# Dealing the merge products differently over eight samples, with one output weight kept in the gates' buffer

## The chip, the cores and the metric

The kernel runs on one core of one Trainium2 chip. The metric is the device time of one execution in microseconds. Before the change three runs took 859.84 us (median), 859.52 and 865.72 us. A separate profiled execution took 862.67 us, with a span of 861.0 us from its first to its last instruction.

## The reference

One inference step of a decoder layer over 272 prompt rows (16 of them meta tokens) and 8 samples of 8 new tokens each. A token mixer has two branches: a recurrent one, A, and softmax attention, B. Each sample attends over 2048 cached positions, which lie in 16 pages. Then comes a mixture of 32 experts, two per token.

```
z = xn @ w_in                                # among others the gates ga, gb: 1024 columns each
merged = sigmoid(ga) * (oa @ proj_a) + sigmoid(gb) * (ob @ proj_b)
h = h + merged @ w_out                       # w_out: 1024 x 1024
h = h + hier_moe(rms_norm(h, ln2_w))         # 32 experts, w1, w3: 1024 x 256, w2: 256 x 1024
y = rms_norm(h, ln_f)
```

The last layer drops the meta tokens, so 256 prompt tokens and 64 sample tokens go through the merge: 320 columns.

## The kernel before

The program is a row of blocks with a barrier between them. This case is about the block `cache` (from L1703), which attends from the samples to their cached pages and, in between, merges the two branches of the prompt. The block after it runs the experts.

**Memory.** One on-chip buffer, `arena`, is cut into weight slots of 128 x 2048 floats (1 MB), named by `place[n]`. The DMA queue of SyncE (SP) fills most of them, and the queue of GpSimd (POOL) loads the cached values. Keys of a sample come as 16 pages of 256 KB into slots 0 to 3 (even samples) or 11 to 14 (odd ones), values as 16 pages into slots 4 to 7. A slot is loaded again as soon as its last reader is done.

**A round of TensorE (PE).** For each sample b the PE queue holds: `scores(b+1)` (L1837, L1854, L1860, L1863); `turn_out(b-1)` (L1912); `turn_probs(b)` (L1880, L1883); `weigh(b)`, the probabilities times the values (L1897, L1906), in four quarters that each wait for four value pages; and then `fills(b+1)`, some of the merge products. In the last round, b = 7, the fills stand ahead of `weigh(7)` instead, behind four turns of the sample tokens' gates (L1980).

**The merge products.** There are 32, in the order of the list `kinds`: 8 of kind "a" (320 columns, four matmuls each, L1938), gated with A's gates into `mT`; 8 of kind "b" (256 columns), gated with B's gates and added to `mT`; 16 of kind "o" (two matmuls of 512 columns in the program, L1927), a quarter of `w_out` (c = 0 to 3) times `mT`, added to `h2`. A float32 matmul of the program is two in the trace, so a product of kind "a" or "b" counts x8 there and one of kind "o" x4. They alternate between two banks of PSUM, so product f waits until VectorE (DVE) has emptied product f-2; the semaphore is `fill_sb`. `turn_probs(b)` uses the same banks and waits for all products so far. `m_ready` counts finished columns of `mT`; the first "o" product waits for all eight.

The table `fill_no` deals them out; its line before, L1676, is `fill_no = [0, 0, 5, 8, 11, 14, 18, 24, 28, len(kinds)]`. `fills(n)` runs the products from entry n to entry n+1, so the rounds get 5, 3, 3, 3, 4, 6, 4 and 4 of them, the last four in round 7.

**DVE** works in a fixed order as well: for sample b the maxima of the scores (L2255), `turn_bias` (L2174), `keep_out(b-2)` (L2213, on which `weigh(b-1)` waits), two key transposes for b+1 (L1590), the sums of the exponentials once ScalarE (ACT) is done with them (L2272), `scale_out(b-1)` (L2206), the outputs of the products `fills_out(b)` (L2239 for "a", L2241 and L2243 for "b", L2233 for "o"), and two transposes for b+2.

**The gates.** The pre-sigmoid gates wait in DRAM as `gates_dram`, (2, 128, 8, 320). `gates_load(a)` brings one branch's into `gates`, 128 x 2560 floats, 10 KB in a row; ACT applies the sigmoid (L2082) in its own order, between the probabilities of sample b and the exponentials of b+1 (L2112), for b = 0 and b = 2. POOL keeps the sample tokens' part aside (L1812) behind its last value pages; PE's turns at L1980 wait for that.

**Output weights.** `out_load(c)` (L1605) brings quarter c of `w_out` into slot 16, 10, 0 or 1. Slots 0 and 1 hold keys of sample 6 until `scores(6)`. The same four slots serve once more at L2039, for the sample tokens.

**After the rounds.** PE turns the normalised tokens (`turn_x2`, L1994), computes the router and the samples' part (L2008 to L2039) and enters the expert block, where 81 more loads of 1 MB run through the slots; `ahead(sp, s)` has filled the 18 slots before with the first expert weights.

Of the kernel before, what the change touches and what calls it, by code (L numbers as in the profile page):

```python
# [12 lines left out]
DM, SEQ, NMETA, HD = 1024, 256, 16, 64  # L13
# [12 lines left out]
P = 128  # L26
# [4 lines left out]
TM = T - NMETA  # L31
# [9 lines left out]
SLOTS, SLOT = 8, 2048  # L41
# [54 lines left out]
def build(nc, A, O):  # L96
# [17 lines left out]
    with ctx:  # L114
# [21 lines left out]
        xnT = keep(KT, T)  # L136
# [1470 lines left out]
        gates = xnT.rearrange("p k t -> p (k t)")[:, 0:DM // P * TM].rearrange("p (d t) -> p d t", d=DM // P)  # L1607
# [68 lines left out]
        fill_no = [0, 0, 5, 8, 11, 14, 18, 24, 28, len(kinds)]  # L1676
# [7 lines left out]

        def out_fill(c):

            return full[out_slot[c]], (48, 16, kneed(6, 0) + 16, kneed(6, 1) + 16)[c]
# [17 lines left out]
        with nc.Block("cache") as block:  # L1705
            @block.sync
            def _(sp):
# [9 lines left out]
                def gates_load(a):  # L1717
                    sp.dma_start(gates, gates_dram[a]).then_inc(S("gates_in"), 16)
# [22 lines left out]
                key_loads(6)  # L1741
                out_load(sp, 0)
                out_load(sp, 1)
                key_loads(7)
                sp.wait_ge(S("sco_ps"), DB - 1)
                out_load(sp, 2)
                out_load(sp, 3)
# [26 lines left out]
            def _(pool):  # L1774
# [37 lines left out]
                nc.gpsimd.tensor_copy(gs_keep, gates[:, :, SEQ:TM].rearrange("p (h k) t -> p k h t", h=2)).then_inc(S("gs_kept"), 1)  # L1812
# [12 lines left out]
            def _(pe):  # L1825
# [89 lines left out]
                def fill(f):  # L1915
# [5 lines left out]
                    if kind == "o":  # L1921
# [3 lines left out]
                        w = place[out_slot[c]].rearrange("p (k n) -> p k n", k=2)  # L1925
# [109 lines left out]
                pe.wait_ge(S("sb_sb"), 1)  # L2035
                for k in range(KT):
                    w = place[out_slot[k // 2]].rearrange("p (k n) -> p k n", k=2)
                    for half, r in enumerate((UP, DN)):
                        mm = nc.tensor.matmul(bank[2][r, :], mT[:, k, SEQ:TM], w[:, k % 2, half * HALF:(half + 1) * HALF],  # L2039
                                              start=(k == 0), stop=(k == KT - 1))  # L2040
# [38 lines left out]
            def _(act):  # L2079
                def gates_on(n):  # L2080
                    act.wait_ge(S("gates_in"), 16 * n)
                    nc.scalar.activation(gates, gates, ACT.Sigmoid).then_inc(S("gates_on"), 1)  # L2082
                    nc.scalar.activation(small[:, 224:225], ones[:, 0:1], ACT.Exp)
# [75 lines left out]
            def _(dve):  # L2159
# [61 lines left out]
                def fill_out(f):  # L2221
# [16 lines left out]
                    if kind == "a":  # L2238
                        TT(mT[:, d, :], out[:, 0:TM], gates[:, d, :], mult).then_inc(S("fill_sb"), 1)  # L2239
                    else:  # L2240
                        ch(TT(btmp, out[:, 0:SEQ], gates[:, d, 0:SEQ], mult))  # L2241
# [681 lines left out]
```

## Time and profile before

| what | value |
|---|---|
| median of three runs | 859.84 us |
| profiled execution, its own time | 862.67 us |
| its span | 861.0 us |
| busy PE / DVE / ACT / POOL | 761.1 / 382.5 / 186.4 / 145.3 us |
| bytes moved, mean rate | 220.26 MB, 256 GB/s |
| cache block, from PE's L1837 of sample 1 to its last L2059 | 406.3 to 626.5 us |
| expert block | 628.7 us to the end |

A row of a timeline gives the start in us, the duration of a merged run of equal instructions, the engine, the line, the operation, `out<-in` by name, and xcount. In brackets stands the idle time of the engine before it and what ended it. "issue" means that the profile names no releaser. In a `--windows` row PEclk is the clock granted to TensorE, as a share of full speed.

### The profile page before, as it was taken

Reading aid. Unit: us, or ns where it says so; the run is one execution under the profiler, and the core shown is the slowest. Engines: PE = TensorE matmul, PEld = TensorE weight load, DVE = VectorE, ACT = ScalarE, POOL = GpSimd, SP = SyncE. Lnnn points to the kernel's source line nnn. Section 1 sums busy time; section 2 is a strip of 40 time slices with the busy share of each in tenths; the row PEclk is TensorE's granted clock in tenths of the full one; section 3 lists DMA queues with packets and bytes.
Section 4 is the critical chain, followed back from the end, with each engine's and each line's share of the span. In section 5 each row is a group of like instructions: output and inputs, shape, how many; then the busy total and the mean of one; then the engine's idle time right before and its main releaser. Section 6 shows DMA issues by size and latency. Waiting matters only on the chain. (4 is left out here: it accounts for less than half of the span.)

```text
span 861.0 us, 20782 instructions
## 1 busy us (share of the span) xinstructions
PE 761.1 (88%) x8681; PEld 445.5 (52%) x8681; DVE 382.5 (44%) x722; ACT 186.4 (22%) x433; POOL 145.3 (17%) x294
## 2 busy tenths in 40 slices
PE   5999999998989999768898997889889987899985
PEld 2445666675666667624565664455644425444421
DVE  2222623228963174748666774633552222422213
ACT  2101321216332210031422320223111110111103
POOL 8500120007020020031504343422000000000000
PEclk9999999988999989768899998999989998999997
DMA  8721431211332113459899999988939999999993
GB/s 311 284 86 54 190 117 49 97 53 67 103 85 84 32 55 85 105 163 396 364 352 414 397 397 409 362 313 314 422 153 425 421 425 421 426 420 425 421 412 121
DMA packets 54647, 220.26 MB, mean 256 GB/s; under 512 B 21935, under 2 KB 24026, under 8 KB 30746
## 3 DMA queue, kind: packets, MB, share of 16 engines
q1 hardware_dynamic: 46576, 183.28, 54.5%
q0 software_dynamic: 7328, 35.48, 10.7%
q8 instruction: 68, 1.11, 0.5%
q10 hardware_dynamic: 650, 0.18, 0.1%
q14 instruction: 25, 0.20, 0.1%
HBM read 211.82 MB, written 7.09 MB: 254 GB/s over the span
## 5 line engine op out<-in xcount | busy, mean ns | idle before, releaser
L232 PE MATMUL bank<-arena 128*128 128x320 f32 x256 | 85.0, 469 | 3.1 <-DVEq L2200 1.8
L208 POOL DMA_DIRECT2D arena<-in_cv x116 | 59.9, 516 | 113.1 <-PE bank L1897 80.8
L513 PE MATMUL bank<-arena 128*128 128x512 f32 (+1 forms) x144 | 69.9, 624 | 1.4 <-DMA arena<-in_w_zb 1.4
L2508 PE MATMUL bank<-arena 128*32 128x512 f32 x512 | 65.4, 624 | 3.3 <-DMA arena<-in_w_exp 2.1
L2739 DVE TENSOR_TENSOR arena<-arena,bank 128x512 f32<-128x512 f32 x35 | 24.1, 687 | 97.2 <-PE bank L2478 94.2
L548 PE MATMUL bank<-arena 128*128 128x336 f32 x224 | 66.3, 450 | 0.6 <-ACT arena L429 0.6
L1590 DVE STREAM_TRANSPOSE arena<-arena 128x2048 f32<-128x2048 f32 x28 | 63.1, 2288 | 4.3 <-DMA arena<-in_ck 2.9
L232 PEld LDWEIGHTS bank<-arena 128*128 128x128 f32 x256 | 47.5, 199 | 24.8 <-issue 7.6
L1897 PE MATMUL bank<-arena 128*16 128x128 f32 x1024 | 35.6, 300 | 19.7 <-issue 11.4
L548 PEld LDWEIGHTS bank<-arena 128*128 128x128 f32 x224 | 41.5, 189 | 21.4 <-issue 1.7
L1389 ACT ACTIVATE arena<-bank 128x384 f32<-128x384 f32 (+6 forms) x63 | 25.1, 444 | 108.2 <-PE bank L232 31.9
L1897 PEld LDWEIGHTS bank<-arena 128*16 128x16 f32 x1024 | 31.3, 106 | 23.4 <-issue 13.4
L2508 PEld LDWEIGHTS bank<-arena 128*32 128x32 f32 x512 | 16.1, 114 | 46.2 <-issue 39.1
L2121 ACT ACTIVATE arena<-bank 128x256 f32<-128x256 f32 x32 | 12.3, 384 | 126.4 <-PE bank L1880 125.6
L2478 PE MATMUL bank<-arena 128*128 128x512 f32 x72 | 37.1, 643 | 2.1 <-ACT arena L2630 0.8
L1854 PE MATMUL bank<-arena 32*16 32x512 f32 x1024 | 38.3, 591 | 0.0
L513 PEld LDWEIGHTS bank<-arena 128*128 128x128 f32 (+1 forms) x144 | 24.2, 184 | 25.5 <-issue 25.5
L1938 PE MATMUL bank<-arena 128*128 128x320 f32 (+1 forms) x128 | 36.3, 444 | 0.0
L2561 PE MATMUL bank<-arena 128*32 128x512 f32 x256 | 30.1, 608 | 5.7 <-ACT arena L2670 5.7
L2469 PE MATMUL bank<-arena 128*128 128x128 f32 x256 | 32.7, 289 | 0.0
L2469 PEld LDWEIGHTS bank<-arena 128*128 128x128 f32 x256 | 31.2, 202 | 1.1 <-issue 0.2
L1938 PEld LDWEIGHTS bank<-arena 128*128 128x128 f32 x128 | 26.1, 209 | 9.4 <-issue 2.8
(495 smaller groups left out, 1103.4 us busy)
## 6 DMA issues: line engine op xcount, KB each, us to landing
arena<-in_w_exp SPq DMA_DIRECT2D x95, 1024.0 KB, 19.1
arena<-in_ck SPq DMA_DIRECT2D x120, 256.0 KB, 6.6
arena<-in_cv POOLq DMA_DIRECT2D x116, 256.0 KB, 7.6
arena<-in_w_gate SPq DMA_DIRECT2D x8, 1024.0 KB, 4.8
arena<-in_w_za SPq DMA_DIRECT2D x7, 1024.0 KB, 6.9
arena<-in_w_zb SPq DMA_DIRECT2D x6, 1024.0 KB, 15.7
arena<-in_w_proj SPq DMA_DIRECT2D x8, 512.0 KB, 9.9
arena<-in_w_out SPq DMA_DIRECT2D x4, 1024.0 KB, 10.6
```

The costliest lines, as they stand in the source:

```text
L208: eng.dma_start(tile[n:P:4, :], src[bass.ds(page, 1)].rearrange("a (p j) n -> (a p) (j n)", j=4))\
L232: mm = nc.tensor.matmul(bank[b][:, 0:TM], w[:, k, a, :], xnT[:, k, NMETA:T], start=(k == 0), stop=(k == KT - 1))
L513: mm = nc.tensor.matmul(bank[q % 6][0:n, :], xnT[:, k, i * P:i * P + n], w[:, k % 4, :], start=(k == 0), stop=(k == KT - 1))
L548: mm = nc.tensor.matmul(bank[j % 2][:, 0:T], w[:, k, (j % 2) * P:(j % 2 + 1) * P], xnT[:, k, :], start=(k == 0), stop=(k == KT - 1))
L1590: return nc.vector.transpose(tile, tile)
L1854: mm = nc.tensor.matmul(bank[i][32 * g:32 * g + 2 * DS, :], qs[r, b, j, :], keys[b % 2][r, :, j, :], start=False, stop=(t == 3))
L1897: mm = nc.tensor.matmul(bank[7][32 * g:32 * g + 2 * DS, 0:P], pT[:, n, 2 * DS * g:2 * DS * (g + 1)], page_part(slot[4 + m], n % 4)[:, g * ...
L1938: mm = nc.tensor.matmul(out[:, 0:nt], w[:, d4, k, :], src[:, k, :], start=(k == 0), stop=(k == 3))
L2469: mm = nc.tensor.matmul(bank[half][:, k * P:(k + 1) * P], x2[:, 2 * i + half, k * P:(k + 1) * P], lhs_sel[:, i, :], start=False, stop=(k = ...
L2478: return nc.tensor.matmul(dst[:, :], gT[:, i, :], yg[:, half * HALF:(half + 1) * HALF], start=True, stop=True)
L2508: mm = nc.tensor.matmul(bank[2][j * CAP:(j + 1) * CAP, :], xg[:, q % 2, k, j * CAP:(j + 1) * CAP], place[s][:, (k % 4) * 512:(k % 4 + 1) * ...
L2561: mm = nc.tensor.matmul(bank[4 + half][j * CAP:(j + 1) * CAP, :], hT[:, f, j * CAP:(j + 1) * CAP], place[s][:, f * DM + half * 512:f * DM ...
```

## The change

`fill_no` becomes `[0, 0, 6, 8, 12, 17, 22, 27, len(kinds), len(kinds)]`: the rounds get 6, 2, 4, 5, 5, 5, 5 and 0 products. Quarter 2 of `w_out` now goes for the prompt into `spare`, which is the first 2048 columns of the gates' buffer once all gates are used. It is loaded a second time, into slot 0, for the sample tokens. To make that slot contiguous, the gates' buffer is split into a prompt part (8 x 256 columns) and a sample part (8 x 64 columns), each loaded by its own DMA. Quarters 0 and 1 are loaded before the keys of sample 6 instead of after them, and quarter 3 before quarter 2.

```diff
+        gates_all = xnT.rearrange("p k t -> p (k t)")[:, 0:DM // P * TM]
+        gates = gates_all[:, 0:SLOT].rearrange("p (d t) -> p d t", d=DM // P)
+        gates_s = gates_all[:, SLOT:].rearrange("p (d t) -> p d t", d=DM // P)
+        spare = gates_all[:, 0:SLOT]
...
-        fill_no = [0, 0, 5, 8, 11, 14, 18, 24, 28, len(kinds)]
+        fill_no = [0, 0, 6, 8, 12, 17, 22, 27, len(kinds), len(kinds)]
...
+        out_tile = [place[out_slot[0]], place[out_slot[1]], spare, place[out_slot[3]]]
...
+            if c == 2:
+                return S("spare_in"), 16
+            return out_full(c)
...
-                    sp.dma_start(gates, gates_dram[a]).then_inc(S("gates_in"), 16)
+                    sp.dma_start(gates, gates_dram[a, :, :, 0:SEQ]).then_inc(S("gates_in"), 16)
+                    sp.dma_start(gates_s, gates_dram[a, :, :, SEQ:TM]).then_inc(S("gates_in"), 16)
...
                 key_loads(5)
-                key_loads(6)
                 out_load(sp, 0)
                 out_load(sp, 1)
+                key_loads(6)
+                sp.wait_ge(S("m_ready"), ND)
+                sp.dma_start(spare, A["w_out"][2]).then_inc(S("spare_in"), 16)
                 key_loads(7)
                 sp.wait_ge(S("sco_ps"), DB - 1)
+                out_load(sp, 3)
                 out_load(sp, 2)
-                out_load(sp, 3)
...
-                        w = place[out_slot[c]].rearrange("p (k n) -> p k n", k=2)
+                        w = out_tile[c].rearrange("p (k n) -> p k n", k=2)
...
                 pe.wait_ge(S("sb_sb"), 1)
+                pe.wait_ge(*out_full(2))
...
-                    act.wait_ge(S("gates_in"), 16 * n)
-                    nc.scalar.activation(gates, gates, ACT.Sigmoid).then_inc(S("gates_on"), 1)
+                    act.wait_ge(S("gates_in"), 32 * n)
+                    nc.scalar.activation(gates_all, gates_all, ACT.Sigmoid).then_inc(S("gates_on"), 1)
...
                     if kind == "a":
-                        TT(mT[:, d, :], out[:, 0:TM], gates[:, d, :], mult).then_inc(S("fill_sb"), 1)
+                        ch(TT(mT[:, d, 0:SEQ], out[:, 0:SEQ], gates[:, d, :], mult))
+                        ch(TT(mT[:, d, SEQ:TM], out[:, SEQ:TM], gates_s[:, d, :], mult))
+                        dve.sem_inc(S("fill_sb"), 1)
```

In PE's queue the end of the cache block reads as follows before the change, from `weigh(6)` to the first rows behind `weigh(7)` (L1897 and L1906 are `weigh`, L1927 the products of kind "o", L1912 `turn_out`, L1880 and L1883 `turn_probs(7)`, L1980 the turned gates, L1994 `turn_x2`).

```order
L1897 MATMUL bank<-arena 16x128 x64
L1906 MATMUL bank<-arena 16x128 x4
L1927 MATMUL bank<-arena 128x512 x8
L1912 MATMUL bank<-arena 128x64
L1880 MATMUL bank<-arena 128x128 x16
L1883 MATMUL bank<-arena 8x64
L1980 MATMUL bank<-arena 128x128 x4
L1927 MATMUL bank<-arena 128x512 x8
L1897 MATMUL bank<-arena 16x128 x64
L1906 MATMUL bank<-arena 16x128 x4
L1994 MATMUL bank<-arena 128x128 x8
```

And with the change, from the same place (all lines are 15 to 16 higher: L1912 and L1921 are now `weigh`, L1942 the products, L1927 `turn_out`).

```order
L1912 MATMUL bank<-arena 16x128 x64
L1921 MATMUL bank<-arena 16x128 x4
L1942 MATMUL bank<-arena 128x512 x10
L1927 MATMUL bank<-arena 128x64
L1895 MATMUL bank<-arena 128x128 x16
L1898 MATMUL bank<-arena 8x64
L1995 MATMUL bank<-arena 128x128 x4
L1912 MATMUL bank<-arena 16x128 x64
L1921 MATMUL bank<-arena 16x128 x4
L2009 MATMUL bank<-arena 128x128 x8
```

Nothing stands between the turned gates and `weigh(7)` any more, and five products instead of four follow `weigh(6)`.

In DVE's queue the second round's products before the change (L2206 is `scale_out(1)`, L2239 the gating of a product of kind "a", L1590 the key transposes behind it):

```order
L2272 TENSOR_REDUCE arena<-arena 128x1
L2274 RECIPROCAL arena<-arena 128x1
L2206 TENSOR_SCALAR arena<-bank,arena 128x128
L2239 TENSOR_TENSOR arena<-bank,arena 128x320 x3
L1590 STREAM_TRANSPOSE arena<-arena 128x2048 x2
```

With the change, at the same place:

```order
L2290 TENSOR_REDUCE arena<-arena 128x1
L2292 RECIPROCAL arena<-arena 128x1
L2222 TENSOR_SCALAR arena<-bank,arena 128x128
L2255 TENSOR_TENSOR arena<-bank,arena 128x256
L2256 TENSOR_TENSOR arena<-bank,arena 128x64
```

The pair L2255 and L2256 stands there twice, for two products, and in the round before six times; the transposes follow.

## Rows read from the trace of the kernel before

**Rows 1.** The page, PE in part 1 and the clock in part 2.
```profile
PE 761.1 (88%) x8681; PEld 445.5 (52%) x8681; DVE 382.5 (44%) x722; ACT 186.4 (22%) x433; POOL 145.3 (17%) x294
...
PEclk9999999988999989768899998999989998999997
```

**Rows 2.** DMA queues in 640 to 845 us: packets, MB, share of 16 engines.
```profile
q1 hardware_dynamic: 13503, 85.28, 100.1%
```

**Rows 3.** A window of 4 us: its length, then PE, PEld, DVE, ACT, POOL busy, clock, DMA share, GB/s.
```profile
628.00:632.00 4.00, 2.13 (x20) 1.84 (x24) 3.03 (x14) 1.18 (x3) 0.00 (x0) 0.56 0.00 0
```

**Rows 4.** PE's timeline, rounds 0 to 2.
```profile
420.76 1.91 PE L1897 MATMUL bank<-arena 128*16 128x128 f32 x32 [3.24 <-DMA arena<-in_cv]
...
452.33 6.73 PE L1938 MATMUL bank<-arena 128*128 128x320 f32 x24
...
473.58 1.07 PE L1897 MATMUL bank<-arena 128*16 128x128 f32 x32 [1.33 <-DMA arena<-in_cv]
...
474.92 5.67 PE L1938 MATMUL bank<-arena 128*128 128x256 f32 x24
```

**Rows 5.** PE's timeline, round 4.
```profile
520.11 1.91 PE L1897 MATMUL bank<-arena 128*16 128x128 f32 x32 [3.51 <-DMA arena<-in_cv]
522.50 5.49 PE L1938 MATMUL bank<-arena 128*128 128x256 f32 x16
529.23 3.67 PE L1927 MATMUL bank<-arena 128*128 128x512 f32 x8 [1.24 <-DVEq L2244]
```

**Rows 6.** Windows of 4 us, columns as above.
```profile
492.00:496.00 4.00, 4.00 (x88) 3.86 (x91) 4.00 (x2) 1.93 (x8) 1.40 (x3) 0.58 0.76 281
...
516.00:520.00 4.00, 0.60 (x24) 0.31 (x12) 2.48 (x4) 0.00 (x0) 2.12 (x6) 0.91 1.03 416
520.00:524.00 4.00, 3.89 (x44) 2.55 (x45) 0.35 (x1) 0.00 (x0) 2.46 (x5) 0.50 1.00 414
```

**Rows 7.** PE's timeline, `weigh(6)` to L2008.
```profile
568.82 3.68 PE L1897 MATMUL bank<-arena 128*16 128x128 f32 x127 [1.37 <-issue]
...
573.28 7.13 PE L1927 MATMUL bank<-arena 128*128 128x512 f32 x16
...
585.10 0.63 PE L1980 MATMUL bank<-arena 128*128 128x128 f32 x4 [1.22 <-POOL arena L1812]
585.56 7.03 PE L1927 MATMUL bank<-arena 128*128 128x512 f32 x16
592.53 3.69 PE L1897 MATMUL bank<-arena 128*16 128x128 f32 x128
596.14 0.41 PE L1906 MATMUL bank<-arena 8*16 8x128 f32 x8
...
598.71 3.65 PE L2008 MATMUL bank<-arena 128*64 128x512 f32 x16
```

**Rows 8.** POOL's timeline, the value pages of samples 4 and 7 and the copy.
```profile
505.26 2.24 POOL L208 DMA_DIRECT2D arena<-in_cv x4 [1.35 <-issue]
...
570.55 2.25 POOL L208 DMA_DIRECT2D arena<-in_cv x4 [10.76 <-PE bank L1897]
...
584.33 0.62 POOL L1812 COPY arena<-arena 128x512 f32<-128x512 f32 x1
```

**Rows 9.** The tile in_cv in 560 to 600 us.
```profile
DMA to landing us min/median/max: 5.8/8.4/10.1
```

**Rows 10.** Timelines of ACT and DVE: second gates, then first squares and last norm.
```profile
470.48 2.34 ACT L2082 ACTIVATE arena<-arena 128x2560 f32<-128x2560 f32 x1 [1.47 <-DMA arena<-gates_dram]
...
478.06 0.41 DVE L2241 TENSOR_TENSOR arena<-bank,arena 128x256 f32<-128x256 f32 x1
...
590.05 1.06 ACT L2135 ACTIVATE arena<-arena 128x1024 f32<-128x1024 f32 x1 [2.18 <-DVE arena L2233]
...
595.86 1.29 DVE L2297 SCALAR_TENSOR_TENSOR arena<-arena 128x1024 f32<-128x1024 f32 x1
```

**Rows 11.** DMA queues in 340 to 352 us, where 256-byte rows are stored.
```profile
q1 hardware_dynamic: 2616, 0.54, 26.1%
```

More of the change, by code:

```diff
@@ L1605, in out_load @@
             sp.dma_start(place[s], A["w_out"][c]).then_inc(full[s], 16)
-        gates = xnT.rearrange("p k t -> p (k t)")[:, 0:DM // P * TM].rearrange("p (d t) -> p d t", d=DM // P)
+        gates_all = xnT.rearrange("p k t -> p (k t)")[:, 0:DM // P * TM]
+        gates = gates_all[:, 0:SLOT].rearrange("p (d t) -> p d t", d=DM // P)
+        gates_s = gates_all[:, SLOT:].rearrange("p (d t) -> p d t", d=DM // P)
+        assert DM // P * SEQ == SLOT
+        spare = gates_all[:, 0:SLOT]
         valid = ident.rearrange("p (g c) -> p g c", g=NPAIR)[:, :, 0:2 * DS]
@@ L1683, in proj_fill, with out_full @@
             return full[proj_slot[2 * a + h]], 32 * (1 + (2 * a + h == 3))
+        out_tile = [place[out_slot[0]], place[out_slot[1]], spare, place[out_slot[3]]]
         def out_fill(c):
+            if c == 2:
+                return S("spare_in"), 16
+            return out_full(c)
+        def out_full(c):
             return full[out_slot[c]], (48, 16, kneed(6, 0) + 16, kneed(6, 1) + 16)[c]
@@ L1811, in _ @@
                 pool.wait_ge(S("sco_ps"), DB)
-                nc.gpsimd.tensor_copy(gs_keep, gates[:, :, SEQ:TM].rearrange("p (h k) t -> p k h t", h=2)).then_inc(S("gs_kept"), 1)
+                nc.gpsimd.tensor_copy(gs_keep, gates_s.rearrange("p (h k) t -> p k h t", h=2)).then_inc(S("gs_kept"), 1)
                 for i in range(8):
@@ L2238, in fill_out @@
                     if kind == "a":
-                        TT(mT[:, d, :], out[:, 0:TM], gates[:, d, :], mult).then_inc(S("fill_sb"), 1)
+                        ch(TT(mT[:, d, 0:SEQ], out[:, 0:SEQ], gates[:, d, :], mult))
+                        ch(TT(mT[:, d, SEQ:TM], out[:, SEQ:TM], gates_s[:, d, :], mult))
+                        dve.sem_inc(S("fill_sb"), 1)
                     else:
-                        ch(TT(btmp, out[:, 0:SEQ], gates[:, d, 0:SEQ], mult))
+                        ch(TT(btmp, out[:, 0:SEQ], gates[:, d, :], mult))
                         dve.sem_inc(S("fill_sb"), 1)
```

## The prediction

> **What bounds the kernel now.** I read the page first: TensorE (PE) is busy 88% of the span [rows 1], so no single wait decides everything, and the question is what binds in the block that changes and in the one behind it. Next the DMA view of the expert block: from 640 to 845 us one queue fills all 16 engines, at 100.1% [rows 2], so that block lasts as long as its loads. It cannot absorb or return anything by itself; what matters is when it starts. Just before it the DMA engines are idle, 0 GB/s in 628 to 632 us [rows 3], because the first expert weights have filled every slot long before. So whatever the cache block gains or loses in PE's order arrives at the end of the run one for one.
>
> Inside the cache block PE's timeline is nearly closed: scores, turned probabilities, `weigh`, products, scores again. The reader is to see there only the idle times in brackets: waits of the last `weigh` quarter for value pages in rounds 0, 2 and 4 (3.24, 1.33 and 3.51 us) [rows 4, 5], a wait of 1.24 for the last column of `mT` [rows 5], and 1.22 for POOL's copy of the sample gates in round 7 [rows 7]. Besides these there is a wait of about 2 us ahead of every `weigh`, which the rows show as 1.37 in round 6 [rows 7]; `keep_out` on DVE ends it, and the change leaves its place in both orders alone.
>
> The third thing to read is the clock. After the 3.51 us wait PE was granted 0.50 in 520 to 524 us, half speed, that is 1.2 instead of 2.4 GHz, after a stretch of 4 us in which it was busy for 0.60 [rows 6]. Two products of kind "b" took 5.49 us there [rows 5], against 5.67 for three of them elsewhere [rows 4].
>
> **The change, part by part.** The same 32 products run, with the same matmuls. One of kind "a" costs 6.73 / 3 = 2.24 us, one of kind "b" 5.67 / 3 = 1.89 [rows 4], one of kind "o" 7.03 / 4 = 1.76 [rows 7]. Moving them costs and gives nothing by itself; the sum is one of waits, after minus before.
>
> 1. *The values of sample 4.* Their last four pages had been issued by 505.26 + 2.24 = 507.50 [rows 8] and let PE go on at 520.11 [rows 5], 12.6 us later; PE needed them 3.51 us earlier, 9.1 us after the issue. The fourth batch of products now has five instead of three: one "b", one "o" and the wait for `mT`, 1.89 + 1.76 + 1.24 = 4.9 us more between issue and need, so 14.0 us against 12.6. Two of the 1 MB loads of `w_out` leave this stretch too, and one enters. The wait goes: -3.51. With it goes the half clock: 5.49 - 2 x 1.89 = 1.7, and 1.91 instead of 1.07 for the quarter itself [rows 4, 5], 0.8. Together -6.0. If the wait stays, 0. The 1.24 itself only moves.
> 2. *The values of sample 2.* Round 1 gets two products of kind "a" instead of three, and round 0 one more. `weigh(1)`, which releases these pages, comes 2.24 us later, their use does not. The wait of 1.33 [rows 4] grows: +2.2, or 0 if the pages move faster than before.
> 3. *The second gates.* ACT waited 1.47 us for them and began the sigmoid at 470.48; DVE reached the first product output of that round at 478.06 [rows 10], because the exponentials stand behind the sigmoid. Two banks let PE run only two products ahead, and it was just not held. Now the load is 1024 rows of 1 KB and 1024 of 256 B instead of 128 of 10 KB. No row has such a load, so I bound it. Stores of 256 B took 0.261 x 16 x 12 us / 2616 = 19 ns each [rows 11], against 256 B at the full rate of 26.5 B/ns, 9.7 ns (414 to 426 GB/s over 16 engines, the DMA rate of the saturated windows [rows 6]). So the 256 B part costs 64 x 9 ns = 0.6 us more per engine, and the 1 KB part between 0 and as much again: +0.6 to +1.2, I take 0.9. Backlog from item 2 adds 0 to 2.2, I take 1.5. DVE then starts at 480.5 instead of 478.1, PE comes 2.2 later itself, and 0.6 is left: +0.6. The upper end is a rival.
> 4. *POOL's copy.* PE reaches the turns of the gates one "o" product later than before, 1.78 us after its old arrival, while the copy stays tied to `weigh(6)`. The 1.22 goes, some 0.3 of waiting for ACT's last copy of probabilities stays: -0.9.
> 5. *The values of sample 7.* The 7.03 us of products behind L1980 [rows 7] covered this load. POOL had issued the last pages by 584.33, when the copy behind them began, [rows 8], and pages landed 5.8 to 10.1 us after issue, median 8.4 [rows 9]: I take 591.0, bounds 589.6 to 593.9. PE without the cover: `weigh(6)` ends at 573.28, five products 8.9, the stretch from the end of the products to the end of L1883 3.5, turned gates 0.8, three quarters 2.8: it asks for the last pages at 589.3. Wait +1.7, bounds 0.3 to 4.6.
> 6. *The norms.* `turn_out(7)` waits for DVE, which first writes two normalised tiles; from the first square to the end of the second tile it took 597.15 - 590.05 = 7.1 us [rows 10], 1.6 of it behind the products that now come earlier. With a table load ahead, the second tile would be done about 7.6 us after L1980, 0.7 behind PE. +0.7, bounds 0 and 1.5.
> 7. *Costed at nothing.* The second load of quarter 2, 1 MB or 2.5 us of all engines, falls where DMA has gaps (item 1's stretch got lighter, and nothing waits on slot 0 until L2039); without the cover it would be 2.5. SyncE's new wait for `m_ready` holds up the keys of sample 7, but those wait for `scores(5)`, which PE runs behind the products that set `m_ready`. The split gating adds a short DVE instruction to each of eight products, at most some 0.4 us per product under PE's 2.24 [rows 4]. The first gates: 0, bounds -1 and +2, since value pages and gates compete there and the one's gain is the other's loss.
>
> The sum: -6.0 + 2.2 + 0.6 - 0.9 + 1.7 + 0.7 = **-1.7 us**. The profiled execution took 862.67, so it would be 861.0; the median of the runs is 2.83 below it, which gives **858.1**.
>
> A page would price item 3 otherwise. The Trainium skill, page "DMA: Bandwidth & Descriptors", section "Why small descriptors are slow (HBM only)", gives a 256 B descriptor 11 cycles where 8 would do, so 27% of overhead. By that the 256 B part would cost an estimated 0.2 us more rather than 0.6. I stay with the row, which holds everything that such a packet costs.
>
> **The rivals.**
>
> *Faster: the clock comes back.* Windows such as 492 to 496 us at 0.58 [rows 6] follow short waits of PE and cost 0.42 x 4 = 1.7 us; the page's clock line shows several slices at 0.8 or less in this block [rows 1]. Other round lengths may spare two of them (-3.4) and items 2 and 3 may not come (-2.8): -7.9, so 851.9. Against it: the waits of 2 us that precede such windows all stay. Chance 0.16.
>
> *Slower: the gates fall behind the values.* If the engines serve the two queues by turns, packet against packet, the gates' small packets now move 1 KB while POOL's value pages move their 8 KB rows. The second half of sample 2's pages, 2 MB or 4.9 us at 424 GB/s, would then go ahead of the gates: 0.9 + 2.2 + 4.9 = 8.0 us late, the sigmoid at 478.5, and everything on DVE behind the exponentials with it. PE's third product of the round waits 8.0 - 2.2 - 0.4 = 5.4 instead of 0.6. The values then come on time (-2.2 of item 2), but a wait of that length brought the half clock in round 4, 2.5 us. In all -1.7 + 4.8 - 2.2 + 2.5 = +3.4, so 863.2, up to 866 if the first gates suffer likewise. It decides from a landing of about 474 us on. For it: ACT already waits for this load, and every DMA engine is taken in those windows. Against it: the bytes in front of it may be small by then. Chance 0.20.
>
> This is what a rule of the Trainium skill would make of the split: "DMA: Bandwidth & Descriptors", section "Queues, rings and completion order", says that each engine goes round the queues it has work for by whole packets. No row here shows the turns.
>
> *Slower: sample 4's pages stay late.* They share the engines with the keys of sample 7 and the new load into `spare`. If those take the whole 4.9 us, item 1 gives nothing: +4.3, so 864.1. It decides if the pages take over 14.0 us. Chance 0.10.
>
> *Nothing:* the waits moved cancel, 859.8. Chance 0.06.
>
> **The numbers.** The forecast has 0.48. Its own range, from the bounds of items 3, 5 and 6 and one clock window either way, is 854.5 to 862. The range for 8 in 10 takes in most of the rivals: 852.5 to 865. A measurement of this kernel tells about 1%, 8.6 us, from no change. Over 1% faster is below 851.2, the outer half of the first rival: 0.08. Over 1% slower is above 868.4, which needs two slower cases together: 0.05. Within: 0.87.
>
> **What the profile will show.** Right: no wait for in_cv in round 4 and two full-speed products behind it; round 2's wait for in_cv near 3.5; a sigmoid at 472 to 474; L1980's turns without a wait for POOL; a wait of 0.3 to 4.6 us in the last quarter of `weigh(7)`; and L2008 some 2 us earlier. Wrong: a sigmoid beyond 474 with PE waiting for DVE in that round; a `weigh(7)` that waits more than 4.6 us for values; or an expert block that does not follow the shift.

## The result, and the profile after

| kernel | median us | runs |
|---|---|---|
| before | 862.78 (859.52 to 867.46) | 4 |
| after | 873.34 (869.08 to 877.92) | 4 |

The ratio is 1.0134, with a 95% interval of 1.0087 to 1.0181. Ratios, here and below, are worked out from the single executions with the slow ones left out, and so differ a little from the quotients of the medians. A second comparison, `after_again` below, gave 1.0077 (1.0033 to 1.0121). The change costs about 1%. The forecast of 858.1 and the range up to 865 were both wrong, on the slower side. The profiled execution of after took 869.08 us, its span 867.5 us against 861.0. From the cache block on, the lines of after are 15 to 18 higher than before.

The page of after. What answers to [rows 1] has not moved:
```profile
PE 761.7 (88%) x8681; PEld 447.3 (52%) x8681; DVE 383.8 (44%) x730; ACT 185.8 (21%) x433; POOL 145.5 (17%) x294
...
PEclk9999999999999969778899899998979998999998
```
PE does the same work. What was added is idle time and work at half clock, at two places. Rows below are one profile of each kernel; the starts in them count from the first instruction, and `scores(1)` began at 406.31 us before and at 407.98 after.

**The first place: round 2.** PE's timeline of after, where [rows 4] is that of before. L1912 is `weigh`, L1953 the "a" and "b" products:
```profile
421.27 1.06 PE L1912 MATMUL bank<-arena 128*16 128x128 f32 x30 [2.07 <-DMA arena<-in_cv]
...
470.73 5.19 PE L1912 MATMUL bank<-arena 128*16 128x128 f32 x128 [1.97 <-issue]
...
476.19 3.72 PE L1953 MATMUL bank<-arena 128*128 128x256 f32 x16
485.48 6.40 PE L1953 MATMUL bank<-arena 128*128 128x256 f32 x16 [5.57 <-DVEq L2260]
```
`weigh(2)` no longer waits for values. But after two products of round 2 (x16), PE stands for 5.57 us until DVE has emptied a bank, and the next two take 6.40 us. DVE waited for ACT, and ACT for the gates. The timelines of ACT and DVE, to be laid beside [rows 10]:
```profile
477.37 2.34 ACT L2098 ACTIVATE arena<-arena 128x2560 f32<-128x2560 f32 x1 [7.05 <-DMA arena<-gates_dram]
```
```profile
484.18 0.16 DVE L2290 TENSOR_REDUCE arena<-arena 128x1 f32<-128x5 f32 x1 [8.95 <-ACT arena L2128]
...
484.95 0.41 DVE L2259 TENSOR_TENSOR arena<-bank,arena 128x256 f32<-128x256 f32 x1
```
DVE reaches the first bank at 484.95 instead of 478.06, 5.2 us later when both are counted from `scores(1)`. SyncE issued the second gates at about the same place in the block, at 461.22 and 461.83 against 459.66 before. The view of DMA issues in 455 to 480 us (the last number is the time from issue to landing) of before:
```profile
arena<-gates_dram SPq DMA_DIRECT2D x1, 1280.0 KB, 10.8
```
And of after, the two parts:
```profile
arena<-gates_dram SPq DMA_DIRECT2D x1, 1024.0 KB, 14.1
arena<-gates_dram SPq DMA_DIRECT2D x1, 256.0 KB, 15.5
```
What happened on the DMA engines meanwhile stands in the rows by queue. q1 is SyncE's queue, with the gates and keys, q0 is POOL's, with the value pages; the columns are packets, MB and share of the 16 engines. Of before, in 466 to 468 us:
```profile
q1 hardware_dynamic: 53, 0.50, 59.1%
q0 software_dynamic: 56, 0.32, 39.9%
```
And of after, in 468 to 470 us:
```profile
q0 software_dynamic: 131, 0.72, 86.4%
q1 hardware_dynamic: 127, 0.14, 19.0%
```
In these stretches the engines serve about as many packets of one queue as of the other. With the small pieces SyncE's packets carry 0.14 MB instead of 0.50, and POOL's pages take the engines.

**The middle: round 4.** What answers to [rows 5] is as forecast, no wait for values ahead of five full-speed products:
```profile
527.60 5.36 PE L1912 MATMUL bank<-arena 128*16 128x128 f32 x128 [1.98 <-issue]
...
533.22 8.85 PE L1942 MATMUL bank<-arena 128*128 128x512 f32 x20
```

**The second place: `weigh(7)`.** PE's timeline where [rows 7] is that of before:
```profile
580.47 8.85 PE L1942 MATMUL bank<-arena 128*128 128x512 f32 x20
...
593.13 0.63 PE L1995 MATMUL bank<-arena 128*128 128x128 f32 x4 [0.35 <-ACT arena L2141]
593.68 1.94 PE L1912 MATMUL bank<-arena 128*16 128x128 f32 x64
598.20 1.07 PE L1912 MATMUL bank<-arena 128*16 128x128 f32 x32 [2.57 <-DMA arena<-in_cv]
602.42 1.91 PE L1912 MATMUL bank<-arena 128*16 128x128 f32 x32 [3.15 <-DMA arena<-in_cv]
...
604.81 1.97 PE L2009 MATMUL bank<-arena 128*128 128x128 f32 x8
...
607.91 3.65 PE L2023 MATMUL bank<-arena 128*64 128x512 f32 x16
```
The turned gates now wait 0.35 for ACT and not 1.22 for POOL. But `weigh(7)` waits twice, 5.72 us in all, and its last quarter and the first turns run at half clock. Windows of 4 us of after, columns as in [rows 3]:
```profile
484.00:488.00 4.00, 2.52 (x6) 2.08 (x7) 2.28 (x7) 0.15 (x2) 2.58 (x5) 0.51 1.01 422
...
528.00:532.00 4.00, 4.00 (x95) 4.00 (x89) 4.00 (x2) 1.59 (x7) 2.08 (x4) 0.57 0.74 217
...
588.00:592.00 4.00, 3.19 (x20) 2.10 (x19) 1.38 (x4) 0.77 (x2) 2.21 (x5) 1.00 1.03 295
...
600.00:604.00 4.00, 1.58 (x32) 1.18 (x32) 1.65 (x4) 0.20 (x1) 0.00 (x0) 0.52 1.01 419
604.00:608.00 4.00, 4.00 (x36) 3.17 (x30) 0.73 (x3) 0.60 (x1) 0.00 (x0) 0.63 1.01 420
```
The granted clock falls to 0.51 and 0.52, 1.2 instead of 2.4 GHz, when PE starts again after the wait of round 2 and after the second wait of `weigh(7)`. The quarter between the two waits still ran at full clock, in 1.07 us. In 588 to 592 us the DMA engines are full (1.03) and yet move only 295 GB/s. The pages of sample 7 that were issued from 582 us on landed late; the tile in_cv in 582 to 600 us, to be laid beside [rows 9]:
```profile
DMA to landing us min/median/max: 8.5/9.1/10.5
```

**The balance in us**, counted from the start of `scores(1)` (406.31 before, 407.98 after). That start is 1.67 later through blocks that the change does not touch.

| stretch | before | after | difference |
|---|---|---|---|
| `scores(1)` to `weigh(7)` | 186.22 | 185.70 | -0.52 |
| `weigh(7)` to the router (L2008, now L2023) | 6.18 | 14.23 | +8.05 |
| the whole | 192.40 | 199.93 | +7.53 |
| expert block to the end of the span | 232.3 | 229.6 | -2.7 |

The first line is itself a sum of gains and losses: in round 2 a wait of 5.57 and half clock of 6.40 - 3.78 = 2.62, against value waits that went or shrank (3.24 - 2.07 = 1.17, 1.33, 3.51), 1.7 of half clock on the products of round 4 and 0.87 at the turned gates. That gives -0.4. Behind the small rest stand larger shifts of the clock that nearly cancel: `weigh(2)` took 5.19 us instead of 2.81 + 1.07, `weigh(3)` 3.69 instead of 5.35, `weigh(4)` 5.36 instead of 2.81 + 1.91. I did not trace them one by one. The last line is hardly an effect of the change: in the eleven other profiles of this study, two of them of kernels like before in all but the gates' load and its gating, the expert block took 229.2 to 230.7 us, so the 232.3 of before's profile stands alone.

### The profile page after: what moved, and what is told of

It is laid out like the page before. It is cut to its first block and busy times, and to the rows that moved or that the text cites. A ratio compares the mean times of both kernels' runs of the same rounds, so it can differ in the third digit from the quotient of the medians.

```text
span 867.5 us, 20802 instructions
## 1 busy us (share of the span) xinstructions
PE 761.7 (88%) x8681; PEld 447.3 (52%) x8681; DVE 383.8 (44%) x730; ACT 185.8 (21%) x433; POOL 145.5 (17%) x294
## 5 line engine op out<-in xcount | busy, mean ns | idle before, releaser
L232 PE MATMUL bank<-arena 128*128 128x320 f32 x256 | 86.8, 478 | 3.8 <-PEq L112 2.0
L1590 DVE STREAM_TRANSPOSE arena<-arena 128x2048 f32<-128x2048 f32 x28 | 63.1, 2288 | 4.9 <-DMA arena<-in_ck 3.7
L232 PEld LDWEIGHTS bank<-arena 128*128 128x128 f32 x256 | 48.5, 203 | 25.7 <-issue 9.3
L1912 PE MATMUL bank<-arena 128*16 128x128 f32 x1024 | 36.2, 303 | 19.9 <-issue 11.9
L548 PEld LDWEIGHTS bank<-arena 128*128 128x128 f32 x224 | 41.5, 189 | 21.4 <-issue 1.7
L1912 PEld LDWEIGHTS bank<-arena 128*16 128x16 f32 x1024 | 31.7, 107 | 23.1 <-issue 13.3
L1953 PE MATMUL bank<-arena 128*128 128x320 f32 (+1 forms) x128 | 37.7, 458 | 5.6 <-DVEq L2260 5.6
L2496 PE MATMUL bank<-arena 128*128 128x512 f32 x72 | 35.3, 616 | 2.2 <-ACT arena L2648 0.8
L1953 PEld LDWEIGHTS bank<-arena 128*128 128x128 f32 x128 | 27.2, 217 | 15.3 <-DVEq L2260 6.0
L2487 PEld LDWEIGHTS bank<-arena 128*128 128x128 f32 x256 | 31.0, 202 | 1.1 <-issue 0.2
## 6 DMA issues: line engine op xcount, KB each, us to landing
arena<-in_w_zb SPq DMA_DIRECT2D x6, 1024.0 KB, 14.8
arena<-in_w_out SPq DMA_DIRECT2D x5, 1024.0 KB, 10.5
arena<-in_w_proj SPq DMA_DIRECT2D x8, 512.0 KB, 10.8
```

What stands on the lines that cost most here:

```text
L232: mm = nc.tensor.matmul(bank[b][:, 0:TM], w[:, k, a, :], xnT[:, k, NMETA:T], start=(k == 0), stop=(k == KT - 1))
L548: mm = nc.tensor.matmul(bank[j % 2][:, 0:T], w[:, k, (j % 2) * P:(j % 2 + 1) * P], xnT[:, k, :], start=(k == 0), stop=(k == KT - 1))
L1590: return nc.vector.transpose(tile, tile)
L1912: mm = nc.tensor.matmul(bank[7][32 * g:32 * g + 2 * DS, 0:P], pT[:, n, 2 * DS * g:2 * DS * (g + 1)], page_part(slot[4 + m], n % 4)[:, g * ...
L1953: mm = nc.tensor.matmul(out[:, 0:nt], w[:, d4, k, :], src[:, k, :], start=(k == 0), stop=(k == 3))
L2487: mm = nc.tensor.matmul(bank[half][:, k * P:(k + 1) * P], x2[:, 2 * i + half, k * P:(k + 1) * P], lhs_sel[:, i, :], start=False, stop=(k = ...
```

## The experiments

The first theory, **G**: the gates' load lost its place among the DMA engines because its pieces shrank from 10 KB to 1 KB and 256 B, while POOL's value pages kept their 8 KB rows. Its rival: it is the deal 6, 2 that puts more value pages in front of the gates, and the pieces matter little. For `weigh(7)`, theory **W**: the loads issued before its last pages share the engines with them, and no product covers them any more; theory **P**: it is the expert prefetches into slots 4 to 7 alone; theory **V**: sample 7's pages are slow by themselves.

**b_split**: the kernel before with the split buffer, the split load and the split gating, and nothing else.
```diff
-                    sp.dma_start(gates, gates_dram[a])
+                    sp.dma_start(gates, gates_dram[a, :, :, 0:SEQ])
+                    sp.dma_start(gates_s, gates_dram[a, :, :, SEQ:TM])
```


> The kernel before with one part of the change alone: the gates' buffer split into a prompt part and a sample part, each loaded by its own DMA (1024 pieces of 1 KB, 1024 of 256 B), and the gating of kind a in two instructions. The deal of the products and all other loads stay. Theory G (small pieces lose their turns to the value pages): the second sigmoid starts some 5 to 7 us later than the 470.5 of before, PE waits 4 to 6 us for DVE at the third product of round 2 and runs at half clock behind it, so the whole is 5 to 8 us slower than before. Rival Q (the load is late in the changed kernel because more is queued in front of it, not because of its pieces): sigmoid within 1.5 us of before, time within 1 us.

Measured: 870.57 us against 866.26, ratio 1.0028 (0.9995 to 1.0062). PE's timeline, rounds 2 and 4:
```profile
485.96 2.45 PE L1941 MATMUL bank<-arena 128*128 128x256 f32 x8 [3.03 <-DVEq L2247]
...
530.00 1.91 PE L1900 MATMUL bank<-arena 128*16 128x128 f32 x32 [4.01 <-DMA arena<-in_cv]
```
The wait for DVE comes with the split alone, though 3.03 us are less than the 4 to 6 expected. As a time the split alone is not told from before: the interval contains 1, where 5 to 8 us were expected. The values of sample 4 stay late, so it was the deal that cured those.

**b_pieces**: the kernel before with 16 unused floats at the end of each row of `gates_dram`. One load, one buffer, one gating as before, but pieces of 1280 B instead of 10 KB.
```diff
-        gates_dram = nc.dram_tensor("gates_dram", (2, P, DM // P, TM), f32, kind="Internal").ap()
+        gates_dram = nc.dram_tensor("gates_dram", (2, P, DM // P, TM + 16), f32, kind="Internal").ap()
```


> The kernel before with padding between the eight rows of a partition's gates in DRAM, so that the one DMA that loads them moves 1024 pieces of 1280 B instead of 128 of 10 KB. Nothing else changes: the bytes, the number of DMAs, the buffers and the gating are those of before. Theory G: the second gates take 12 to 16 us from issue to landing instead of 10.8, and PE waits 1 to 5 us for DVE in round 2. Rival: only the 256 B pieces or the second DMA of the split cost, and the gates land within 11.5 us.

Measured in one run: 870.18 us. The second gates in the DMA issues, the queues in 472 to 474 us, then PE's timeline:
```profile
arena<-gates_dram SPq DMA_DIRECT2D x1, 1280.0 KB, 14.0
```
```profile
q0 software_dynamic: 125, 0.66, 81.4%
q1 hardware_dynamic: 124, 0.16, 21.4%
```
```profile
487.63 2.00 PE L1938 MATMUL bank<-arena 128*128 128x256 f32 x8 [3.04 <-DVEq L2242]
```
The same 1.25 MB, in the same order of everything, takes 14.0 us instead of 10.8. The number of loads, the 256 B pieces and the split gating are not needed for it: the size of the pieces is enough. And the queues show how. As many packets of the gates as of the value pages are served (124 and 125), but one of the gates is 0.16 MB / 124 = 1.3 KB, a single piece, and their queue gets 21% of the engines instead of 59%.

**a_packed**: after, with the gates packed in DRAM in the order of the split buffer, so that one load of 10 KB rows fills both parts; the stores are split instead.
```diff
-                    sp.dma_start(gates, gates_dram[a, :, :, 0:SEQ])
-                    sp.dma_start(gates_s, gates_dram[a, :, :, SEQ:TM])
+                    sp.dma_start(gates_all, gates_dram[a])
```


> The changed kernel with the gates laid out in DRAM as the split buffer needs them (each product of the gates is stored by two DMAs, 128 x 256 and 128 x 64), so that one DMA loads them in rows of 10 KB again. Theory G: the second sigmoid starts at 471 to 473 us instead of 477.4, PE's wait of 5.6 us for DVE in round 2 is at most 1 us, and 5 to 8 us of the loss of the changed kernel go; some 2.5 to 5 us slower than before remain, from the end of the block. Rival Q: the sigmoid still starts after 475 us and less than 2 us is won.

Measured: 867.68 us, ratio 1.0016 (0.998 to 1.0051). The second gates, and PE's timeline in round 2:
```profile
arena<-gates_dram SPq DMA_DIRECT2D x1, 1280.0 KB, 13.3
```
```profile
476.11 1.90 PE L1917 MATMUL bank<-arena 128*16 128x128 f32 x32 [3.18 <-DMA arena<-in_cv]
```
PE waits no more for DVE. It waits for values instead, which is item 2 of the prediction (3.5 forecast). And the load took 13.3 us even with big rows, which hints, in one profile, that the deal 6, 2 has its part too. `weigh(7)` kept its waits (1.88 and 3.52). The time is not told from before all the same, so the gates in one piece give back most of the loss; how much exactly is open, since the intervals of this ratio and of after_again's (1.0033 to 1.0121) just overlap.

**a_late**: after, with the prefetches into slots 4 to 7 held back until `weigh(7)` is done.
```diff
-                for m in range(4):
-                    sp.wait_ge(S("pv_ps"), 4 * (DB - 1) + m + 1)
-                    ahead(sp, 4 + m)
+                sp.wait_ge(S("pv_ps"), 4 * DB)
+                for m in range(4):
+                    ahead(sp, 4 + m)
```


> The changed kernel, with SyncE's four prefetches into slots 4 to 7 held back until weigh(7) is done, instead of one behind each of its quarters. Theory P (in the changed kernel the prefetches that the first quarters of weigh(7) release run beside the last value pages and take half of the engines): the two waits of 2.6 and 3.2 us in weigh(7) shrink to 0.5 to 2.5 together, and 3 to 6 us against the changed kernel are won. Rival V (the pages are late because POOL issues them late, whoever else loads): the waits stay at 5 us or more, and the time stays or grows by up to 2 us.

Measured: 870.7 us, ratio 1.0056 (1.0018 to 1.0094). PE's timeline:
```profile
600.57 1.07 PE L1912 MATMUL bank<-arena 128*16 128x128 f32 x32 [2.24 <-DMA arena<-in_cv]
604.23 1.91 PE L1912 MATMUL bank<-arena 128*16 128x128 f32 x32 [2.59 <-DMA arena<-in_cv]
```
4.83 us of wait against 5.72 (5.68 in after_again): P, which wanted 0.5 to 2.5, falls. Those prefetches cost at most 0.9.

**a_cover**: after, with four products put back ahead of `weigh(7)`.
```diff
-        fill_no = [0, 0, 6, 8, 12, 17, 22, 27, len(kinds), len(kinds)]
+        fill_no = [0, 0, 6, 8, 12, 16, 20, 24, 28, len(kinds)]
```


> The changed kernel with another deal: 6, 2, 4, 4, 4, 4, 4 and 4 products, so that four of kind o stand ahead of weigh(7) again as before. Split gates, spare slot and second load stay. Theory C (the products ahead of weigh(7) cover the last value pages and the prefetches): no wait in weigh(7), L2023 follows L1995 as closely as L2008 follows L1980 before, and 6 to 8 us are won at that place; round 2's wait for the gates, 5.6 us, stays, so 0 to 4 us slower than before. Rival D (the deal in the middle rounds is what costs): the loss stays at 8 us or more.

Measured: 866.22 us, ratio 0.9997 (0.996 to 1.0034). PE's timeline:
```profile
485.15 3.72 PE L1953 MATMUL bank<-arena 128*128 128x256 f32 x16 [2.58 <-DVEq L2260]
527.14 1.07 PE L1912 MATMUL bank<-arena 128*16 128x128 f32 x32 [1.48 <-DMA arena<-in_cv]
...
583.92 0.63 PE L1995 MATMUL bank<-arena 128*128 128x128 f32 x4 [0.90 <-POOL arena L1827]
594.44 1.07 PE L1912 MATMUL bank<-arena 128*16 128x128 f32 x32 [0.28 <-DMA arena<-in_cv]
```
The cover is worth most of the loss: the waits of `weigh(7)` shrink to 0.28, from its start to the router it takes 7.16 us instead of 14.23, and the time is that of before, though the gates are late. Two things keep this from being the whole loss by itself. The deal of the middle rounds changed with it, and in this profile the gates were less late than in the four others with the same load and the same deal of rounds 0 and 1 (PE's wait 2.58 against 4.19 to 6.08). And a_packed came almost as near to before without any cover. The waits for POOL (0.90) and for sample 4 (1.48) come back in part.

**after_again** and **a_hold**, run beside each other: after unchanged, and after with all eight prefetches, those into slots 11 to 14 too, held back until `weigh(7)` is done.
```diff
-                for s in (11, 12, 13, 14):
-                    ahead(sp, s)
...
+                sp.wait_ge(S("pv_ps"), 4 * DB)
+                for s in (11, 12, 13, 14, 4, 5, 6, 7):
+                    ahead(sp, s)
```


> The changed kernel itself once more, beside the others of this set on the same chip, as the base for them. Both theories: 4 to 11 us slower than before, with the same three places as in its first trace: 4 to 7 us of ACT's waiting for the second gates, 3 to 6 us of PE's waiting for DVE in round 2, and 4 to 6 us of waiting for values in weigh(7).

> The changed kernel with the four prefetches into slots 11 to 14 (4 MB, issued by SyncE once scores(7) is done) held back until weigh(7) is over, together with those into slots 4 to 7. Theory W (these 4 MB and the small-row loads behind them stand in the engines' way when the last value pages come, so every page takes 8 to 10 us): pages of sample 7 land within 3 to 6 us of their issue, the two waits in weigh(7), 5.7 us in the changed kernel, fall to less than 1.5 together, and L2023 comes 5 to 8 us earlier after L1995. Whether the time follows depends on the 8 MB of prefetch that now start later: they have some 40 us until the first expert, enough for 16 MB, so 3 to 7 us won; a loss if they are late. Rival V (POOL's issue alone makes the pages late): the waits stay at 4 us or more.

Measured: after_again 872.6 us, ratio 1.0077 (1.0033 to 1.0121); a_hold 872.09, ratio 1.005 (1.0007 to 1.0093). The profile of after_again has after's waits again: ACT 5.84 for the second gates, PE 4.19 for DVE in round 2 and 5.68 in `weigh(7)`. The pages of sample 7 (tile in_cv, 579 to 600 us), of after_again:
```profile
DMA to landing us min/median/max: 5.8/8.6/10.0
```
Of a_hold, with PE's timeline and ACT's:
```profile
DMA to landing us min/median/max: 3.2/3.7/5.0
```
```profile
604.47 1.09 PE L2007 MATMUL bank<-arena 128*128 128x128 f32 x8 [1.29 <-DVE arena L2313]
606.72 0.69 PE L1925 MATMUL bank<-arena 128*128 128x64 f32 x2 [1.16 <-DVE arena L2220]
...
609.05 5.49 PE L2021 MATMUL bank<-arena 128*64 128x512 f32 x16
```
```profile
426.86 2.34 ACT L2096 ACTIVATE arena<-arena 128x2560 f32<-128x2560 f32 x1 [12.93 <-DMA arena<-gates_dram]
```
W is right about the pages: with nothing of SyncE's issued beside them they land 3.7 us after issue, and `weigh(7)` has no wait. V falls. (The 4 MB and the small loads behind them are not told apart: with the 4 MB held back the small loads had landed before the last pages were issued.) The next thing late is the norms on DVE (1.29 and 1.16). The medians show almost nothing of the gain, 0.5 us, and the profile shows where it went. From the turned gates to the router it takes 10.45 us against 14.71 in after_again, 4.3 less, but the router's first row ran at half clock (5.49 us against 3.65), as did part of what follows, and from there to the expert block it takes 32.99 against 30.03. So 1.3 us arrive. Apart from that PE waited 10.90 us for DVE in round 0 of this profile, because the first gates took so long; holding back a prefetch at the end of the block can't cause that. Why the first gates vary so, below.

**a_pack53**: a_packed with five products in round 0, three in round 1 and four in each later round.
```diff
-        fill_no = [0, 0, 6, 8, 12, 17, 22, 27, len(kinds), len(kinds)]
+        fill_no = [0, 0, 5, 8, 12, 16, 20, 24, 28, len(kinds)]
```


> The changed kernel with packed gates in DRAM (one load in 10 KB rows), and with the deal 5, 3, 4, 4, 4, 4, 4 and 4. Theory G and C together: no part of the gates' wait of 5.6 us and no wait in weigh(7); values of sample 2 wait 0.5 to 2 us as before the change; values of sample 4 wait 0 to 2. 2 to 6 us faster than before, 8 to 12 us faster than the changed kernel. Rival S (round 2 is short of DMA time whatever the pieces, so that gates or values are late there): a wait of 2 us or more for values in round 2, and a time within 2 us of before.

Measured: 858.88 us against 865.18, ratio 0.9946 (0.9905 to 0.9987). ACT's and PE's timelines:
```profile
471.19 2.34 ACT L2103 ACTIVATE arena<-arena 128x2560 f32<-128x2560 f32 x1 [1.09 <-DMA arena<-gates_dram]
```
```profile
476.16 1.07 PE L1917 MATMUL bank<-arena 128*16 128x128 f32 x32 [1.42 <-DMA arena<-in_cv]
...
571.62 0.28 PE L1917 MATMUL bank<-arena 128*16 128x128 f32 x1 [2.77 <-issue]
...
596.72 3.65 PE L2028 MATMUL bank<-arena 128*64 128x512 f32 x16
```
From `scores(1)` (409.18) to the router it takes 187.54 us against 192.40 before. A wait of 2.77 us ahead of the last matmul of `weigh(6)`, for which the profile names no releaser, is in it; b_split, b_pieces, a_split53 and pack53_again have it too (2.0 to 2.7), before only 0.23, and no run tells what it is.

**a_split53** and **pack53_again**, together on one chip: a_pack53's deal with the gates loaded in two parts as in after, and a_pack53 once more.

> The change with the products dealt 5, 3, 4, 4, 4, 4, 4, 4; the gates are still loaded in two parts (1 KB and 256 B pieces). It differs from a_pack53 in the gates' way through DRAM alone. If the piece size of the gates' load is the cause of the late gates, the second sigmoid begins 4 to 7 us later than in a_pack53 (471.19), at 475 to 478, PE waits 2.5 to 5 us for DVE in round 2, the value waits of rounds 0 and 2 shrink, and the kernel ends 2 to 5 us after a_pack53: a ratio to the kernel before of 0.997 to 1.003. If the deal of round 1 (three products instead of two) alone put it right, the sigmoid is at 471 to 473 and the ratio is a_pack53's, 0.9946. Both expect no wait over 1 us in the last weigh.

> a_pack53 once more, in five rounds instead of three. If its gain is real, the ratio to the kernel before lies again at 0.990 to 0.999, with no wait for DVE's product outputs over 1.5 us in round 2, no value wait in round 4 and none over 1 us in the last weigh. If it was one lucky chip, 1.000 or above.

Measured against 864.72: a_split53 862.84, ratio 0.9957 (0.9918 to 0.9997); pack53_again 859.73, ratio 0.9883 (0.9813 to 0.9953). PE's timeline of a_split53:
```profile
484.95 6.14 PE L1953 MATMUL bank<-arena 128*128 128x256 f32 x16 [3.93 <-DVEq L2260]
...
529.38 1.07 PE L1912 MATMUL bank<-arena 128*16 128x128 f32 x32 [2.05 <-DMA arena<-in_cv]
```
And of pack53_again:
```profile
432.82 6.73 PE L1958 MATMUL bank<-arena 128*128 128x320 f32 x24 [2.57 <-DVEq L2262]
...
501.18 1.07 PE L1917 MATMUL bank<-arena 128*16 128x128 f32 x32 [1.82 <-DMA arena<-in_cv]
```
a_pack53's kernel beats before a second time, in six runs. Its profile does not say where: from `scores(1)` to the router it takes 193.06 us, no less than before's 192.40, with a wait of 2.57 for DVE in round 0 and a new one of 1.82 for values in round 3. The gain rests on the times alone. The split load brings the wait for DVE in round 2 back, but as a time the two variants are not told apart: their intervals overlap, and a_split53 is at 0.9957 where 0.997 to 1.003 was expected. With this deal the small pieces cost a wait that the profile shows and no time that the runs can tell. (The profiled execution of a_split53 took 869.97 us, 7 us above its median.)

The time from issue to landing of the second gates (of the 256 B part where there are two), over all twelve profiles, with the wait for DVE in round 2:

| gates' load | deal of rounds 0 and 1 | landing us | PE's wait for DVE us |
|---|---|---|---|
| 10 KB rows | 5, 3 (before, a_pack53, pack53_again) | 10.8, 10.2, 10.6 | none |
| 10 KB rows | 6, 2 (a_packed) | 13.3 | none |
| small pieces | 5, 3 (b_split, b_pieces, a_split53) | 13.1, 14.0, 14.0 | 3.03, 3.04, 3.93 |
| small pieces | 6, 2 (after, after_again, a_late, a_hold, a_cover) | 15.5, 14.3, 14.8, 14.9, 12.7 | 5.57, 4.19, 6.08, 4.94, 2.58 |

The size of the pieces stands clear of the spread: with the deal 5, 3 small pieces landed after 13.1 to 14.0 us and big rows after 10.2 to 10.8. The deal does not: with small pieces its two groups overlap (13.1 to 14.0, 12.7 to 15.5), and with big rows 13.3 is one profile. PE waits for DVE in round 2 in every profile with small pieces and in none with big rows. In a_packed the values were late as well, and so PE came later itself.

## Why the prediction was wrong, by its steps

The forecast lay 15.2 us below the median. Of these 2.9 are its base: it started from 859.84, and with a fourth run the median of before is 862.78. The working itself gave -1.7 for the cache block, and the block measured +7.5. Up to `weigh(7)` the terms of items 1 to 4 add up to -4.1, and -0.5 was measured; behind it items 5 and 6 give +2.4, and +8.05 was measured. Both stretches failed, the second by more.

1. *Values of sample 4*, -6.0: right in its mechanism, -4.6 in size. The wait is gone in all five profiles with five products there; with four it is 1.48 and 2.05 (none in the two with packed gates), with three 3.51, 4.01 and 4.06. The products behind it are at full speed (8.85 / 5 = 1.77). But `weigh(4)` itself now falls into a window at 0.57 and takes 5.36 us, against 2.81 + 1.91: the half clock moved rather than went.
2. *Values of sample 2*, +2.2: did not come in after, where the wait of 1.33 fell to nothing, because the gates took the delay. With packed gates it came: 3.18 against the 3.5 forecast.
3. *Second gates*, +0.6: **the first step that failed**. The sum priced the small pieces by the bytes' overhead, 0.9, and the backlog at 1.5. (Its own working leaves 2.4 - 2.2 = 0.2 for PE and not 0.6; beside the miss that is nothing.) Measured: pieces +3.2 at the old deal (10.8 to 14.0), backlog +2.8 at big rows (10.5, the mean of three, to 13.3, one profile). The sigmoid began at 477.37, or 475.7 on the clock of before, past the 474 named as the point of decision; the rival "the gates fall behind the values" gave 478.5, a wait of 5.4 and 2.5 of half clock, and the profile has 5.57 and 2.62. I had given it 0.20. The mistake was to ask what the pieces cost and not what turn they get. The queues of before already show the turns, 53 packets of SyncE's to 56 of POOL's in 466 to 468 us. In after it is 127 to 131 in 468 to 470 us, with 0.14 against 0.72 MB, and in b_pieces, with nothing but the piece size changed, 124 to 125, with 0.16 against 0.66. The rule named with that rival is that engines go round their queues by whole packets (the Trainium skill, "DMA: Bandwidth & Descriptors", "Queues, rings and completion order"), and the trace agrees by these counts. A packet of that page is several descriptors, though, and one of the profile a single piece, so how many pieces make one turn stands in no row. The estimate by the overhead that the same page of the Trainium skill gives, 0.2 us, was as far off as mine.
4. *POOL's copy*, -0.9: right, 0.87.
5. *Values of sample 7*, +1.7: **the second step that failed, and the costlier**. The waits are 5.72, beyond the bound of 4.6. The last pages had been issued by 592.01 and let PE go on at 602.42, 10.4 us later, where the sum took 6.7. It gives no reason for that: the bounds are 583.8, the last issue, plus 5.8 and 10.1 [rows 9], and the median of 8.4 would have given 592.2 and a wait of 2.9 instead of 591.0 and 1.7. The median was too low as well, because the pages of that stretch are not alike. PE needs the last ones, and the profile of before has them for 578 to 600 us:
```profile
DMA to landing us min/median/max: 8.2/8.9/10.1
```
   These stand behind 4 MB of prefetch and small loads; their landing in after was 8.5 to 10.5, and 3.2 to 5.0 in a_hold without the prefetch. Half clock in 600 to 608 us adds about 2 (the last quarter 1.91 against 1.07, L2009 1.97 against 1.09), which no term held, although item 1 had just priced the same thing.
6. *Norms*, +0.7: 0 in after, since the values are later than the norms. a_hold, which takes the values away, shows 2.45 of waits, and a_cover 0.39: without cover the term was too small as well, but hidden.
7. *Costed at nothing*: right for the 1 MB load, the wait for `m_ready` and the split gating: no wait names them. The first gates cost no wait of PE in after's profile, but 0.98, 1.40 and 10.90 in a_late, after_again and a_hold, so the +2 I allowed was not enough.

That whatever the cache block gains or loses arrives one for one fits: with the block at +7.5 us the medians differ by 10.6 and, the second time, by 7.4, and in all twelve profiles the stretch from the router to the end of the span took 259.2 to 262.7 us. But the block of a single profile does not stand for the median: a_packed's is 6.2 us longer than before's at a ratio of 1.0016, and a_split53's 8.0 longer at 0.9957. The slower cases were each sized below 1%, and I gave them together 0.05; but a late gates' load and a bare `weigh(7)` came together, and b_split and a_packed show that each comes without the other.

*Open:* the first gates. They landed 6.6 us after issue in before and 6.9 in a_pack53, but 9.8 in a_packed and 11.6 in pack53_again with the same big rows, and 14.4 in b_pieces. What precedes them in the blocks before differs from run to run (`scores(1)` starts anywhere from 404.1 to 412.3), and no experiment separated that from the size of the pieces.

## What to carry to other kernels

Before a change that cuts a load into smaller pieces, look at what the other queues move at that moment: the cost is not in the bytes but in the share of the engines that each turn brings, and whoever waits for that load pays. Work that stands between a load's issue and its use is cover; before moving it, price the load by its last pages with the traffic of that moment, not by a median, and add the half clock that followed waits of 3 us here. And a deal that looks even by counts of products is measured by the waits: five, three and then four each, with the gates in one piece, was 0.5 and 1.2% faster than before in two comparisons.

## What the runs showed of the hardware

- While two queues both had work, the DMA engines served as many packets of one as of the other, whatever their size: 53 and 56 in 2 us of before, 127 and 131 of after, 124 and 125 of b_pieces. The queue with pieces of 1 KB or 1280 B got 19 and 21% of the engines, and 59% with 10 KB rows. Not every window is so even: in 462 to 464 us of before it was 60 and 91.
- Padding a DRAM tensor so that 10 KB rows became pieces of 1280 B made a load of 1.25 MB land after 14.0 instead of 10.8 us beside another queue with 8 KB rows.
- The DMA engines can be full and slow: a share of 1.03 at 295 GB/s in 588 to 592 us of after, where small loads (normalisation rows, router weights) are on the way (in 588 to 590 us 78 packets of SyncE's queue moved 0.12 MB), against 1.01 at 422 GB/s elsewhere. The share alone does not say that bandwidth is used up.
- A page of 256 KB took 3.7 us (median, a_hold) from issue to landing with little beside it but its own kind, and 8.6 us (after_again) with 4 MB and small loads of another queue on the engines.
